# The last token tile of a router table on one core: one table product moved behind the last out-projection, the table's operands in another format, and two weight loads behind a wait

## The reference, cut to what matters

```python
for l in range(DEPTH):                                   # DEPTH = 1, 1024 tokens, D = 1024
    hn = rmsnorm(x, attn_norm_g[l]); proj = hn @ w_in[l] # split into conv, q, k, v, gate parts
    x = x + jnp.concatenate([conv_out, gla_out], axis=-1) @ w_out[l]
    hf = rmsnorm(x, ffn_norm_g[l])
    x = x + hier_moe(hf, ...)                            # top-1 of 4 groups, top-2 of its 8 experts
return rmsnorm(x, final_norm_g)
```

## Time and profile before

| | |
|---|---|
| three runs | 1143.13, 1143.51, 1147.76 us; median 1143.51 us |
| profiled execution | 1147.87 us, span 1146.2 us |
| PE, weight load, DVE, ACT, POOL busy | 95%, 75%, 82%, 61%, 30% of the span |
| mean granted TensorE clock | 0.971 |
| chain that ended last | PE 57%, DVE 2%, DMA 2% |

### The profile page before, as it was taken

How to read it: one execution, slowest core, us unless ns; L and a number is a source line. 1 busy time by engine, 2 the same in 40 slices (tenths; PEclk the granted TensorE clock), 3 DMA queues, 4 the chain that set the end, 5 groups by cost and what they waited for, 6 DMA issues and landing times.

```text
span 1146.2 us, 14763 instructions
## 1 busy us (share of the span) xinstructions
PE 1084.1 (95%) x5072; PEld 863.9 (75%) x5072; DVE 941.6 (82%) x890; ACT 696.2 (61%) x704; POOL 339.5 (30%) x305
## 2 busy tenths in 40 slices
PE   7999999999999985999999999999999999999944
PEld 5758888877788874788888888888888888888821
DVE  5469999783766566799999999999999999999827
ACT  6575464433732231687777777777777777778612
POOL 0267998521200001223212122221222212122113
PEclk9989999999999986899999999999999999999977
DMA  9421110200521134799999999999999999999546
GB/s 324 130 74 31 43 55 20 74 1 1 218 81 69 64 120 178 249 341 378 371 393 367 386 398 401 369 394 376 369 373 364 375 363 366 377 358 362 220 190 254
DMA packets 68342, 283.00 MB, mean 247 GB/s; under 512 B 11760, under 2 KB 30368, under 8 KB 41424
## 3 DMA queue, kind: packets, MB, share of 16 engines
q1 hardware_dynamic: 54384, 255.95, 59.9%
q0 software_dynamic: 10544, 18.08, 4.5%
q10 hardware_dynamic: 3376, 8.47, 1.9%
HBM read 275.64 MB, written 26.74 MB: 264 GB/s over the span
## 4 chain that ended last, share of the span: by engine, by line
PE 57%; DVE 2%; DMA 2%; issue 1%; ACT 0%; SPq 0%; POOL 0%; POOLq 0%; DVEq 0%; ACTq 0%
PE ps L1908 17%; PE ps L1907 17%; PE ps L1906 17%; PE ps L1899 3%; PE ps L1928 1%; PE ps L1975 1%; DVE fin L1595 1%; DMA hf_rows<-hfp 1%; DMA raw<-expert_rows 1%; DMA xg<-hf_rows,idx_g 0%; DVE hfp L1345 0%; PE ps L1824 0%; DMA expert_rows<-ym,now_s 0%; DMA out_dram<-fin 0%; DVE x L1584 0%
## 5 line engine op out<-in xcount | busy, mean ns | idle before, releaser
L1492 DVE TENSOR_TENSOR w_lo<-raw,w_hi 128x2048 fp32r<-128x2048 f32 x206 | 467.7, 2289 | 45.7 <-ACT w_hi L1008 44.3
L1008 ACT ACTIVATE w_hi<-raw 128x2048 fp32r<-128x2048 f32 x206 | 392.1, 1918 | 29.8 <-PE ps L1908 29.8
L1906 PE MATMUL ps<-w_hi,xm_hi 128*128 128x512 f32 x560 | 224.4, 401 | 2.0 <-DVE xm_lo L1505 1.3
L1908 PE MATMUL ps<-w_hi,xm_lo 128*128 128x512 f32 x560 | 224.0, 400 | 0.0
L1907 PE MATMUL ps<-w_lo,xm_hi 128*128 128x512 f32 x560 | 222.7, 398 | 0.0
L1906 PEld LDWEIGHTS ps<-w_hi,xm_hi 128*128 128x128 f32 x560 | 106.0, 189 | 27.1 <-DVE xm_lo L1505 1.6
L1907 PEld LDWEIGHTS ps<-w_lo,xm_hi 128*128 128x128 f32 x560 | 106.3, 190 | 25.5
L1908 PEld LDWEIGHTS ps<-w_hi,xm_lo 128*128 128x128 f32 x560 | 105.8, 189 | 23.8
L1906 PE MATMUL ps<-w_hi,hm_hi 128*128 128x512 f32 x280 | 113.0, 404 | 1.8 <-DVE hm_lo L1518 1.5
L1908 PE MATMUL ps<-w_hi,hm_lo 128*128 128x512 f32 x280 | 111.4, 398 | 0.0
L1907 PE MATMUL ps<-w_lo,hm_hi 128*128 128x512 f32 x280 | 110.8, 396 | 0.0
(11 more groups left out here) (319 smaller groups left out, 1893.3 us busy)
## 6 DMA issues: line engine op xcount, KB each, us to landing
raw<-in_expert_w_down_dram SPq DMA_DIRECT2D x70, 1024.0 KB, 7.8
raw<-in_expert_w_up_dram SPq DMA_DIRECT2D x69, 1024.0 KB, 7.6
raw<-in_expert_w_gate_dram SPq DMA_DIRECT2D x68, 1024.0 KB, 7.3
raw<-in_w_in_dram SPq DMA_DIRECT2D x8, 1024.0 KB, 7.2
raw<-expert_rows SPq DMA_DIRECT2D x12, 512.0 KB, 8.2
xa<-in_x_dram SPq DMA_DIRECT2D x8, 512.0 KB, 8.7
raw<-in_w_out_dram SPq DMA_DIRECT2D x4, 1024.0 KB, 6.5
xin<-in_x_dram SPq DMA_DIRECT2D x8, 512.0 KB, 3.4
```

The lines of the kernel that those rows point to most:

```text
L1008: act.activation(w_hi[:, slot, :], raw[:, r, :], ACT.Copy).then_inc(hi_rdy, 1)
L1492: dve.tensor_tensor(w_lo[:, slot, :], raw[:, r, :], w_hi[:, slot, :].bitcast(F32), ALU.subtract)\
L1906: pe.matmul(dst, x_hi, w_hi[:, s, cols], start=first, stop=False)
L1908: return pe.matmul(dst, x_lo, w_hi[:, s, cols], start=False, stop=stop)
```

## The change

Three edits. TensorE makes `table(5)` behind the whole out-projection of the last tile, ahead of `ranks(6)`, and no longer ahead of `logits(6)`. `oneR` and `jcol` are declared in the high-part format, so all 16 table matmuls read them so. VectorE no longer waits for the stored rows ahead of the lists; the SP queue now waits for all eight stores ahead of the two down pieces of expert 0.

```diff
-        oneR = at("oneR", [P, 2, CAP], over=o_q + 12 * D)
-        jcol = at("jcol", [P, 2, NC, NE], over=o_q + 13 * D)
+        oneR = at("oneR", [P, 2, CAP], F32R, over=o_q + 12 * D)
+        jcol = at("jcol", [P, 2, NC, NE], F32R, over=o_q + 13 * D)
...
             sp.wait_ge(yo_ps, NT)
             load_second(0)
             load_second(1)
+            for b in range(2):
+                sp.wait_ge(hf_out[b], 16 * (NT // 2))
             load_first(4)
             load_first(5)
...
-            dve.wait_ge(hf_out[0], 16 * (NT // 2))
-            dve.wait_ge(hf_out[1], 16 * (NT // 2))
             dve.wait_ge(oh_used, 2 * NT)
...
-                if t >= 2:
+                if 2 <= t < NT - 1:
                     table(t - 2)
                 logits(t - 1)
                 if t == NT - 1:
                     out_projection(t, 1, range(2, KC))
+            table(NT - 3)
             ranks(NT - 2)
```

## The result

The changed kernel took 1137.2 us (median of 5 runs, 1133.65 to 1138.86), the kernel before 1143.57 (5 runs beside it, 1143.13 to 1147.76). The ratio is 0.9924, with a 95% interval of 0.9901 to 0.9947: about 8.7 us faster, and clear of the 0.5% that I had set as the border. My 1138.3 us and its range hold the median, but the gain that I had summed against the median was 5.2 us, and I had put more chance on "no change that can be told" (0.53) than on "faster" (0.43). That was wrong, and one step is behind most of it: I took the new format to count at tile 7 alone.

The account below looks back on a forecast made before the run. The prediction took the expert stage as a fixed block, bound by its first matmul's start. Move 4.1 + format and waits 1.5 - gather 0.4 = 5.2 us off the median 1143.5 gave 1138.3 us, range 1135.3 to 1141.8.

Parts of the forecast that it names:

- the expert stage as a fixed block: Expert stage: TensorE has no gap there, so an earlier change counts only by when the first expert matmul starts, 457.88.
- Part 1, the move: Table product of tile 5 behind the out-projection: last residual starts 5.6 us sooner in the profiled execution, 4.1 against the median.
- the middle one of my three cases: TensorE's logits and out-projection: clock falls at 423.3, returns after up to 5 us of gap-free matmuls, done at 429.8.
- VectorE's floor: Ahead of the last residual: VectorE's weight piece and choose(6) leave it free at 429.05, no sooner.
- Part 2, the format: Table products in high-part format: a quarter of the array time, counted only at tile 7, last record about 447.8, not 448.74.
- Part 3: Lists on VectorE wait for the table product, not the last store; 1.5 us won together with the format.
- The gather's price: Gather ahead of the experts: company of the down pieces for some 2 us, taken as 0.4 us, between 0 and 4.6.
- The rival that the gather pays: Gather collides with the down pieces on shared DMA engines, 7.9 instead of 4.4 us; 1141.4 us in all, chance 0.11.
- Nothing moves: Store as late as before and out-projection not sooner, as VectorE's piece and choose(6) end later; 1143 us, chance 0.04.
- slower: Held-back down pieces and expert 1's piece 3 delay TensorE if stores land very late; about 1148 us, chance 0.04.
- The clock keeps the gain: Clock did not fall at tile 7 in median runs, or now costs more; gain 2.8 us, 1140.7 us, chance 0.13.
- The step from profile to median: Profile stands 4.4 us above the median, partly perhaps at tile 7, so the move's 5.6 us became 4.1.

Follow-up runs that it names:

- e2: Kernel before with only table(5) moved behind the last out-projection, plain float32 operands and waits as before; ratio 0.9969.
- e10: The changed kernel run once more, no further edit; ratio to the kernel before 0.9923.
- e4: Changed kernel with the table operands of tiles 0 to 4 back in plain float32; ratio to the kernel before 0.9950.
- e1: Kernel before with only oneR and jcol in the high-part format, order and waits as before; ratio 0.9955.
- e3: Kernel before with only the waits changed: VectorE's removed ahead of the lists, the SP queue's added ahead of the down pieces; ratio 0.9989.
- e6: Changed kernel without the new SP queue wait, VectorE still not waiting; ratio to the kernel before 0.9929.
- e8: Changed kernel with an earlier VectorE weight piece, more out-projection ahead of logits(6), and rank operands in the high-part format; ratio to the kernel before 0.9910.

## Why the prediction was right and wrong

- **What bounds the kernel, and the expert stage as a fixed block: right.** From the first expert matmul to the end of the span it took 688.32 us before and 688.71 after.
- **Part 1, the move: right in mechanism, and in size within its bounds.** Forecast 5.6 us for an execution like the profiled one (bounds 2.7 to 6.2), 5.87 in the changed kernel, with the residual at 13.60 us after the one before it. The clock did fall, as in the middle one of my three cases, and came back after 3.4 us (windows of the changed kernel):

```profile
417.00:417.50 0.50, 0.50 (x4) 0.50 (x4) 0.50 (x3) 0.49 (x1) 0.00 (x0) 0.66 0.97 401
420.50:421.00 0.50, 0.50 (x3) 0.39 (x3) 0.43 (x3) 0.00 (x0) 0.00 (x0) 0.93 0.00 0
```

  VectorE's floor was where I had put it: in e2 and e10 the residual waits for nothing of TensorE and comes 13.22 and 13.24 us after the one before it, where my sum had 13.3. Two readings were off without weight in the sum: TensorE went on 1.5 us after it had stopped (421.44 - 419.91; 1.55 in the changed kernel), not 1.8, and the lower bound is 2.8 by its own terms (435.22 - 432.4).
- **Part 2, the format: the failed step.** I wrote "Only tile 7's product lies on the path". The chain of my window begins at 416.98 us, where the products of tiles 0 to 4 are over, and from there on the sentence holds. But my own show the product of tile 4 at 407.60, with the logits right behind it. Those five tiles make their table products on a TensorE without gaps, and the change is in all of them. I had the price per product (a quarter of the array time) and multiplied it by one tile. e4 measures the missing term by itself: 3.04 us (94.26 - 91.22), and e1 finds it alone, 3.03 us. With it, my sum against the median is 8.2 us, beside the 8.7 of the ratio. At tile 7 the format was worth the 1 us that I had taken.
- **Part 3: right.** The lists won 1.50 us, forecast 1.5. The stall went to the table product, and the store landed in 3.2 us. Format and waits were both needed, as I had written: at the lists the format alone gave nothing (14.19 in e1) and the waits alone 0.1 (14.06 in e3, with a `logits(7)` of 3.0 us in place of 1.95). The 1.5 us are not there in every execution: the same kernel had 13.70 at the lists in e10, where `logits(7)` took 3.6 us.
- **The gather's price, 0.4 us: wrong side.** It took 4.35 us, 4.42 before. The rival that the gather pays did not come: the two pieces were issued at 432.2 and took 7.0 us, so they were done at 439.2, 2 us after the gather's issue at 437.23, and the gather took no longer than without them (4.39 us in e6). What it did in those 2 us the trace does not show. The rule of shared engines, from the Trainium skill's page "DMA: Bandwidth & Descriptors" (section "Issuing engines are not separate DMA queues"), agrees with the store (3.2 us without the down pieces, 9.03 with them in e6); on the gather it shows nothing here.
- **The other rivals.** "Nothing moves" and "slower" fell. "The clock keeps the gain" holds in part: e2 loses 0.6 us to it at `logits(7)`, e10 1.05 us at the lists (13.70 against 12.65), and beside e3, with its shorter low clock, the move wins 4.4 us in the changed kernel and not 5.87.
- **The step from profile to median: right in its place.** I cut part 1 from 5.6 to 4.1 us because the profile stood 4.4 us above the median and I supposed that some of it lay at tile 7. It did: the profile of e3, at 1143.48 us, has 17.98 us from 6 to 7 with the order of before. Beside it the changed kernel's part 1 is 4.38 us. That the 4.1 comes so near is partly luck, since I chose it between 1.3 and 5.6 without a second execution to read it from. The other 2.7 us lie ahead of the first residual, 1.1 of them at 46 us already (46.83 against 45.77 for the same matmul) and the rest where the low clock after 71 us lasts 6.8 and 3.4 us. From e3 to the changed kernel the terms are 0.40 ahead of the first residual (of no edit), 3.04 for the format in tiles 0 to 4, 4.38, 1.41 at the lists, nothing at the gather, and 0.43 lost in the expert stage: 8.8 us between the two spans, beside the 8.7 of the ratio.
- **Between the two profiles that I had.** Of their 13.59 us, 3.12 stood ahead of the first residual and belong to no edit; 3.03 + 5.87 + 1.50 + 0.07 lie behind it, and of the 5.87 some 1.5 are the longer low clock of before.

## What to carry to other kernels

An edit of a declaration or a helper changes every call of it: count the calls in all stages, and for each ask whether its engine has gaps there, before taking the one at the chain's bend as the only one. Cut two profiles at the same events and compare distance by distance; over tiles 0 to 6, where the clock is full and TensorE has no gap, the distances agree to 0.02 us between executions whose whole times differ by 5, so they show a term that the times cannot. Where the clock falls they do not agree: 19.47 and 17.98 us for the same instructions. So take a second execution of the kernel before, and lay its pieces beside the first's, before a saving is read from one profile.

## What the runs showed that I had not expected

- The whole spread of before, 1142.3 to 1148.4 us over the 32 runs beside e1 to e4, lies in two groups, 14 runs up to 1145.3 and 18 from 1147.0. The profiles of before and of e3, one in each group, differ by 4.4 us, and the low clock accounts for most of it: 6.8 against 3.4 us after 71 us, about where TensorE makes eight small matmuls (16 rows of contraction), and 10.2 against 6.8 us at tile 7; another 1.1 us stood at 46 us already. What decides how long it lasts is open; no run changed the first of these stretches.
- A product of 32 columns gains by the format too, though its columns are few: from the start of the two rank products to what follows them it took 0.37 us and takes 0.22 in e8, and the distance of two residuals fell from 14.97 to 14.75 us.
- One 512 KB store took 7.5 to 9.0 us in the five traces where four 1 MB loads were issued 5 to 7 us ahead of it, and 2.6 to 3.4 us in the eight where only two were. In the profile of before it landed at 449.29, a little behind the down pieces (448.0 by their median), though it is half the size of one: the loads ahead of it set when it landed, not its own size.
